# First stage of a hybrid decoder layer: weight splits before swaps and step sizes, V in side banks, stores issued by SyncE

## The reference

```
h = rmsnorm(x) * norm_pre
z, xbc, dt_raw, q, k, v, g_att, b, c, hs, g_sc = split(h @ w_in)
dt = softplus(dt_raw + dt_bias); a_cum = cumsum(dt * -exp(a_log))      # step sizes, 32 heads
k, q = rope(k), rope(q)                                                # 4 key heads, 16 query heads
y_att = window_attention(q, cache_k + k, cache_v + v, sinks) * silu(g_att)
y_ssd = chunked_scan(conv(xbc), dt, a_cum, state) ...
y_sc  = b * conv3(c * hs) * silu(g_sc)
x += rmsnorm(concat(y) @ w_out) * norm_post
x += sigmoid(x @ ple_gate) * (p @ ple_proj)
outputs: x, new conv and scan states, the last 128 keys and values of each sequence
```

## Time and profile before

| | |
|---|---|
| median of 3 runs | 2210.95 us (2208.93 to 2211.19) |
| the profiled execution | 2206.55 us |
| its span, first to last instruction | 2204.7 us |
| TensorE busy | 2108.5 us, 96% |
| VectorE busy | 1404.4 us, 64% |
| ScalarE busy | 1088.7 us, 49% |
| mean granted TensorE clock | 0.985 of full speed |
| memory traffic | 169 GB/s over the span |

### The profile page before, as it was taken

One profiled execution on the slowest core, in us unless ns is written; L12 is line 12 of the kernel. 1 busy time (PEld: TensorE's weight loads), 2 busy tenths in 40 slices (PEclk: granted clock), 3 DMA queues, 4 the chain that ended last, 5 costly groups with the idle time before them and its releaser, 6 DMA issues.

```text
span 2204.7 us, 39574 instructions
## 1 busy us (share of the span) xinstructions
PE 2108.5 (96%) x15750; PEld 2044.0 (93%) x15750; DVE 1404.4 (64%) x2329; ACT 1088.7 (49%) x2151; POOL 53.7 (2%) x141
## 2 busy tenths in 40 slices
PE   4899999999999999999968999999999999999999
PEld 3899999999999989999968999999999998999999
DVE  5476677577677674347564667676776776644575
ACT  4456456446455454345444564563564464533543
POOL 0000000001001000000000000000000000000000
PEclk9999999999999999999989999999999999999999
DMA  5645455455455355554536455454554553555544
GB/s 199 189 138 174 159 182 174 152 180 176 135 204 166 127 198 182 179 175 153 170 121 194 144 164 184 157 174 159 182 174 158 183 178 116 200 179 179 170 154 148
DMA packets 146369, 370.94 MB, mean 168 GB/s; under 512 B 28584, under 2 KB 65256, under 8 KB 144744
## 3 DMA queue, kind: packets, MB, share of 16 engines
q1 hardware_dynamic: 133552, 336.39, 46.3%
q10 hardware_dynamic: 12488, 29.65, 3.9%
q0 software_dynamic: 144, 2.36, 0.3%
HBM read 340.41 MB, written 32.01 MB: 169 GB/s over the span
## 4 chain that ended last, share of the span: by engine, by line
PE 80%; DVE 7%; DMA 5%; ACT 3%; DVEq 2%; SPq 1%; issue 1%; ACTq 1%
PE main L461 24%; PE main L463 23%; PE main L462 23%; DMA raw<-wts 4%; PE yo L587 2%; DVE wlo L1168 1%; PE yb L580 1%; DVE conv_sum L1402 1%; DMA ssm_p<-work 1%; PE yo L585 1%; DVEq L1200 1%; PE t L664 1%; ACTq L804 1%; DVEq L1290 1%; DVEq L1579 1%
## 5 line engine op out<-in xcount | busy, mean ns | idle before, releaser
L461 PE MATMUL main<-h_hi,whi 128*128 128x288 f32 x3952 | 1193.6, 302 | 55.4 <-DVE work L1198 18.6
L462 PE MATMUL main<-h_lo,whi 128*128 128x288 f32 x3952 | 1175.0, 297 | 0.0
L463 PE MATMUL main<-h_hi,wlo 128*128 128x288 f32 x3952 | 1170.8, 296 | 0.0
L1168 DVE TENSOR_TENSOR wlo<-raw,whi 128x1024 fp32r<-128x1024 f32 x568 | 691.8, 1222 | 451.6 <-ACT whi L786 438.7
L461 PEld LDWEIGHTS main<-h_hi,whi 128*128 128x128 f32 x3952 | 749.9, 190 | 77.0 <-issue 28.8
L786 ACT ACTIVATE whi<-raw 128x1024 fp32r<-128x1024 f32 x568 | 577.5, 1053 | 379.9 <-DMA raw<-wts 214.2
L462 PEld LDWEIGHTS main<-h_lo,whi 128*128 128x128 f32 x3952 | 751.5, 190 | 4.2 <-issue 2.7
L463 PEld LDWEIGHTS main<-h_hi,wlo 128*128 128x128 f32 x3952 | 752.8, 190 | 0.0
L1402 DVE SCALAR_TENSOR_TENSOR conv_sum<-conv_in,gpar_sb,conv_sum 128x312 f32<-128x312 f32 x144 | 90.2, 626 | 119.3 <-ACT conv_sum L948 111.3
L462 PE MATMUL main<-yssd_lo,whi 128*128 128x288 f32 x512 | 151.1, 295 | 0.0
L463 PE MATMUL main<-yssd_hi,wlo 128*128 128x288 f32 x512 | 150.9, 295 | 0.0
(11 more groups left out here) (271 smaller groups left out, 1819.1 us busy)
## 6 DMA issues: line engine op xcount, KB each, us to landing
raw<-wts SPq DMA_DIRECT2D x568, 512.0 KB, 3.6
work<-s_t SPq DMA_DIRECT2D x32, 512.0 KB, 6.0
ssm_s<-work ACTq DMA_DIRECT2D x8, 2048.0 KB, 8.0
work<-masks SPq DMA_DIRECT2D x8, 720.0 KB, 4.8
y_or_x<-xs SPq DMA_DIRECT2D x16, 288.0 KB, 4.3
xs<-y_or_x ACTq DMA_DIRECT2D x2, 2016.0 KB, 7.5
y_or_x<-x SPq DMA_DIRECT2D x4, 576.0 KB, 5.5
xs<-y_or_x POOLq DMA_DIRECT2D x1, 2304.0 KB, 7.6
```

The costliest lines, as they stand in the source:

```text
L461: mm(out, w_hi, x_hi_, start=start, stop=False)
L462: mm(out, w_hi, x_lo_, start=False, stop=False)
L463: return mm(out, w_lo, x_hi_, start=False, stop=stop)
L1168: return tt(dst, raw, hi.bitcast(F32), ALU.subtract)
```

## The change

TensorE: units 2 and 3 go to the side banks YB and YO, which the turned V tiles use after them; the main banks pass from K straight to group 0's first two units. ScalarE: halves 5, 6 and 7 are split before it waits for the K pair; then come both swaps, then the halves 8 to 12 with the steps and the V copies between them. VectorE: low parts 4 to 7 first, then both rotations, then the whole of `step_sizes`, then low part 8 and what follows. The K stores, V stores and cache copies are issued by SyncE: K stores after group 0's second unit has been loaded, V stores after the fourth, cache copies after unit 8 of group 1. In group 0 the keys come from `KTT` in SBUF instead of memory, without the waits for `k_stored` and `tok_ready`, one unit earlier; values are loaded after k = 5 there. The step buffers move to where the attention's PR begins, `RST` to the start of the attention region and `HF` behind the step-size weights.

```diff
--- before.py
+++ after.py
@@ -199,21 +199,22 @@
         NM = cut(16)
         DEN = cut(16)
         OS = cut(2 * NSM).rearrange("p (a n) -> p a n", n=NSM)
+        PR_AT = at[0]
         PR = cut(4 * 3 * P).rearrange("p (j n) -> p j n", j=4)
         PS = cut(NB * P + NSM)
         PT = cut(4 * 3 * P).rearrange("p (j n) -> p j n", j=4)
         PTS = cut(9 * P)
 
         XSQ = cut(KT * T, 0)
-        DT0 = cut(T, HEAVY + 2400)
+        RST = cut(T, HEAVY)
+        HF = [cut(T) if i else cut(T, KT * T + DTW) for i in range(6)]
+        DT0 = cut(T, PR_AT)
         AC0 = cut(T)
         W0 = cut(T)
         DTR = cut(T)
         DTE = cut(T)
         DTU = cut(T)
         DTC = cut(T)
-        RST = cut(T)
-        HF = [cut(T) for _ in range(6)]
         assert at[0] <= LATE
         KTT = cut(2 * T, LATE).rearrange("p (t n) -> p t n", n=T)
         KSW = cut(2 * T).rearrange("p (t n) -> p t n", n=T)
@@ -225,7 +226,7 @@
         YLO = post.enter_context(nc.sbuf_tensor("yssd_lo", [P, KT * T], F32R))
         MIX = post.enter_context(nc.sbuf_tensor("mix", [P, KT * T], F32))
         DTRAW = post.enter_context(nc.sbuf_tensor("dt_raw", [P, DTW], F32))
-        assert 3 * KT * T + DTW <= WK_N and LATE >= 2 * KT * T + 7 * T and 2 * KT * T + UNIT - KT * T <= HEAVY + 2400
+        assert 3 * KT * T + DTW <= WK_N and LATE >= 2 * KT * T + 7 * T and 2 * KT * T + UNIT - KT * T  <= WK_N
         PRAW = YX[:, KT * T:KT * T + 2 * T]
 
         COS, SIN = CST[:, C_COS:C_COS + T], CST[:, C_SIN:C_SIN + T]
@@ -255,7 +256,7 @@
                 return L * self.per + (self.pre + G * self.grp + n + 1)
 
         A0, A1 = Bank("a0", 0, 10, 3), Bank("a1", 0, 9, 3)
-        YB, YO = Bank("yb", 1, 7, 3), Bank("yo", 1, 7, 2)
+        YB, YO = Bank("yb", 2, 7, 3), Bank("yo", 2, 7, 2)
         T0, T1 = Bank("t0", 2, 8, 1), Bank("t1", 1, 8, 2)
         BANKS = {"A0": A0, "A1": A1, "T0": T0, "T1": T1}
         SIDE = [A0, A1, YB, YO, T0, T1]
@@ -318,7 +319,7 @@
         def gunit(L, g, k):
             return L * LAYER_U + g * GRP_U + (PRE_U + k)
 
-        OUT_F = PRE_U // 2 + G * GRP_U // 2
+        OUT_F = 1 + G * GRP_U // 2
         E_F = OUT_F + KT // 2
         GATE_F = E_F + 2
 
@@ -392,18 +393,32 @@
                 for g in range(0, G):
                     for k in range(GRP_U):
                         load_unit(gunit(L, g, k))
-                        if k == (1 if g else 2):
+                        if g == 0 and k == 1:
+                            sp.wait_ge(k_ready, L * 2 + 2)
+                            for i in range(2):
+                                sp.dma_start(kout[L, 2 * i:2 * i + 2].rearrange("h d n -> (h d) n"), KTT[:, i, :]).then_inc(k_stored, 16)
+                        if g == 0 and k == 3:
+                            sp.wait_ge(v_tok, L * 2 + 2)
+                            for i in range(2):
+                                for h in range(2):
+                                    v_h = VT[:, i, :].rearrange("p (c h d) -> p c h d", c=3, h=2)[:, :, h, :]
+                                    sp.dma_start(vout[L, 2 * i + h, 0:NPR].rearrange("(c p) d -> p c d", p=P), v_h[:, 0:2]).then_inc(v_stored, 16)
+                                    sp.dma_start(vout[L, 2 * i + h, NPR:T], v_h[0:NSM, 2]).then_inc(v_stored, 16)
+                        if g == 1 and k == 8:
+                            sp.dma_start(kold[L], kc_t[L].rearrange("g d (b w) -> (g d) b w", w=P)[:, :, NS:P]).then_inc(old_copied, 16)
+                            sp.dma_start(vold[L], vc_t[L][:, NS:P, :]).then_inc(old_copied, 16)
+                        if k == 1:
 
                             if L + g > 0:
                                 sp.wait_ge(y_sq, it(L, g - 1, 3, 2))
                             sp.wait_ge(s1_stored, L * (G * 16) + g * 16 + 16)
-                            sp.wait_ge(k_stored, L * 32 + 32)
-                            sp.wait_ge(tok_ready, L + 1)
+                            if g > 0:
+                                sp.wait_ge(k_stored, L * 32 + 32)
                             for r in range(2):
-                                sp.dma_start(KCUR[64 * r:64 * r + 64, :], kout[L, g]).then_inc(att_in, 16)
+                                sp.dma_start(KCUR[64 * r:64 * r + 64, :], kout[L, g] if g else KTT[0:64, 0, :]).then_inc(att_in, 16)
                             sp.dma_start(KC[0:64, :], kc_t[L, g]).then_inc(att_in, 16)
                             sp.dma_start(MSK, masks).then_inc(msk_in, 16)
-                        if k == 3:
+                        if k == (3 if g else 5):
 
                             sp.wait_ge(v_stored, L * 128 + 128)
                             sp.dma_start(VC, vc_t[L, g].rearrange("w (b d) -> w b d", d=HD)).then_inc(val_in, 16)
@@ -503,13 +518,19 @@
                     mm(T1.t[:, 0:T], w, HLO[:, c0:c0 + T], start=False, stop=False)
                     last = mm(T1.t[:, 0:T], wl, HHI[:, c0:c0 + T], start=False, stop=(n == KT - 1))
                 last.then_inc(T1.full, 1)
-                for k in (2, 3):
-                    project(unit(L, k), k % 2, fill(L, k % 2, k // 2))
+                for k, bk in ((2, YB), (3, YO)):
+                    wait(bk.free, bk.in_pre(L, 0))
+                    for n in range(KT):
+                        wait_half(unit(L, k), n)
+                        last = product(bk.t[:, 0:T], unit(L, k), n, HHI, HLO, n, n == 0, n == KT - 1)
+                        if n % 8 == 7:
+                            last.then_inc(halves_used, 1)
+                    pe.sem_inc(bk.full, 1)
 
                 def turn_values(i):
                     bk = (YB, YO)[i]
                     wait(v_ready, L * 2 + (i + 1))
-                    wait(bk.free, bk.in_pre(L, 0))
+                    wait(bk.free, bk.in_pre(L, 1))
                     for c in range(3):
                         n = P if c < 2 else NSM
                         last = tr(bk.t[0:n, c * P:c * P + P], VTT[:, i, c * P:c * P + n], ID)
@@ -589,7 +610,7 @@
                         last.then_inc(YO.full, 1)
 
                     for k in range(GRP_U):
-                        project(gunit(L, g, k), k % 2, fill(L, k % 2, (PRE_U + g * GRP_U + k) // 2))
+                        project(gunit(L, g, k), k % 2, fill(L, k % 2, 1 + (g * GRP_U + k) // 2))
                         if k < 2 and g > 0:
                             late_states(g - 1, k)
                         if g == 0 and k == 0:
@@ -825,14 +846,20 @@
                     fn(HHI[:, i * T:(i + 1) * T], HF[i % 6], ACT.Copy).then_inc(h_hi, 1)
                 act.wait_ge(layer_in, L * 64 + 64)
                 fn(DTP[0:32, 2:3], DTP[0:32, 1:2], ACT.Exp)
-                for k in range(PRE_U):
-                    act.wait_ge(halves_used, used(unit(L, k)))
-                    if k < 2:
-                        swap(KSW[:, k, :], MAIN[k % 2]).then_inc(k_swapped, 1)
-                    else:
-                        fn(VTT[:, k - 2, :], MAIN[k % 2][:, 0:T], ACT.Copy).then_inc(v_ready, 1)
-                        act.drain().then_inc(bank_free[k % 2], 1)
-                    split_after(unit(L, k))
+                def keep_values(i):
+                    bk = (YB, YO)[i]
+                    act.wait_ge(halves_used, used(unit(L, 2 + i)))
+                    fn(VTT[:, i, :], bk.t[:, 0:T], ACT.Copy).then_inc(v_ready, 1)
+                    act.drain().then_inc(bk.free, 1)
+
+                first_half = 2 * unit(L, 0)
+                for h in (5, 6, 7):
+                    split_hi(first_half + h)
+                act.wait_ge(halves_used, used(unit(L, 1)))
+                for k in range(2):
+                    swap(KSW[:, k, :], MAIN[k]).then_inc(k_swapped, 1)
+                for k in range(4):
+                    split_hi(first_half + 8 + k)
                     if k == 0:
 
                         act.wait_ge(dt_abs, L + 1)
@@ -840,6 +867,9 @@
                         act.wait_ge(dt_u, L + 1)
                         fn(DTC[0:32, :], DTU[0:32, :], ACT.Ln).then_inc(dt_ln, 1)
                     if k == 1:
+                        keep_values(0)
+
+                    if k == 2:
 
                         act.wait_ge(ac_ready, L + 1)
                         fn(AC3[0:32, :], AC0[0:32, :], ACT.Copy).then_inc(ac_hi, 1)
@@ -848,21 +878,15 @@
                         fn(AC3[32:64, :], DTR[0:32, :], ACT.Copy).then_inc(ac_mid, 1)
                         act.wait_ge(dt_ac, L + 1)
                         fn(W0[0:32, :], DTE[0:32, :], ACT.Exp, scale=-1.0).then_inc(dt_wexp, 1)
-                    if k == 2:
-                        for i in range(2):
-                            act.wait_ge(k_ready, L * 2 + (i + 1))
-                            act.dma_start(kout[L, 2 * i:2 * i + 2].rearrange("h d n -> (h d) n"), KTT[:, i, :]).then_inc(k_stored, 16)
+                    if k == 3:
+                        keep_values(1)
+                        split_hi(first_half + 12)
 
                 def store_values(i):
                     bk = (YB, YO)[i]
```

(26 more changed lines are left out.)

## The result

Four runs of the changed kernel gave a median of 2196.80 us (2195.25 to 2197.92), four of the kernel before beside them 2211.07 (2208.93 to 2213.00): a ratio of 0.9935, interval 0.9918 to 0.9952. It is faster by 14.3 us, not by 32.6, and 2196.8 lies above the range of 2172 to 2192.

The account below looks back on a forecast made before the run. TensorE was taken as the bound, busy 2108.5 of 2204.7 us. Gains of 15.9 us in layer 0 and 16.7 in layer 1, together 32.6, took 2206.55 to 2174.0, or 2178.4 on the median's footing; range 2172 to 2192.

Parts of the forecast that it names:

- V in side banks: First stage, both layers: units 2 and 3 no longer wait for the main banks; the 4.04 and 1.72 us go.
- the step chain: First stage: step sizes end at 61.5, the product about 67.6, against the turn at 70.3; cost nothing.
- half 8: Group 0's first unit: weight half ready at 62.7, wanted by TensorE at 63.9; slack 1.2 us, the tightest place.
- Rival A: First stage: half 8 late behind the step sizes, 2 to 4 us per layer, 2182 to 2186; chance 0.16.
- B: First scores: ScalarE still late through weight halves queued behind loads and stores; 6 us per layer stay, 2190; chance 0.12.
- Stores to SyncE: Before group 0's first scores: ScalarE's 6.1 us of issue goes, so the 5.32 us gap goes too.
- a part worth nothing: If moving the stores wins nothing: ScalarE 2 to 4 us late for the second swap, time 2182 to 2186.
- Cache copies: Group 1: next half issued at 303.2 lands near 309, harmless until 318.8; ScalarE may wait 1 to 2 us; cost nothing.
- Rival D: Unit 9 of group 1: cache copies starve the weight ring, 18.5 us per layer, 2215 and up; chance 0.04.
- The last sign: First stage: a time above 2192 would mean that a queue, not TensorE, sets it.
- Group 0's keys on chip: Group 0: keys on chip replace a round trip through memory and a wait; counted as nothing.
- the moved buffers: Buffers moved to other places carry no instruction; counted as nothing.

Follow-up runs that it names:

- the GpSimd run: The changed kernel with its two cache copies issued by GpSimd on its own queue instead of SyncE, same place in group 1; 2201.39 us, ratio 0.9962 to the kernel before.

## Why the prediction was wrong

**V in side banks, the step chain, half 8: right.** Half 8's low part was made from 61.6 on (forecast 61.5), unit 2 and unit 3 ran without a gap at clock 1.00, the steps were turned at 70.36 (forecast 70.3), the scores came at 84.52 (84.5), the fourth unit at 85.38 (85.3). Rival A and B had no part. The answering rows of VectorE and SyncE after:

```profile
61.62 2.34 DVE L1189 TENSOR_TENSOR wlo<-raw,whi 128x1024 fp32r<-128x1024 f32 x2
```

```profile
78.75 0.90 SPq L368 DMA_DIRECT2D raw<-wts  x2
```

Half 16 was issued at 78.75, as forecast ("about 79"), and was in time.

**Stores to SyncE: right in time, wrong in cause.** The 5.32 us before the scores did go. I put them down to ScalarE's 6.1 us of issue; with the same issue time back on ScalarE the kernel loses 1.4 us in all, and with the value copy cut otherwise those waits shrink in the old kernel by 3.6 and 4.7 us of 5.32 and 6.16, all its stores still on ScalarE. The issue took the 6 us that I read, but it stood beside other work; most of the wait was the value copy's. My price for a part worth nothing, 4 to 8 us, was too high as well.

**Cache copies: the step that failed.** They were put at "cost nothing" in group 1 and cost 8.1 and 8.5 us. "It would land near 309, behind them", 5.8 us after its issue at 303.2; it landed 15.7 us after, issued at 286.89 in a kernel that was 17 us ahead by then. The two ends stood in the text (309, and 318.8 as the latest harmless moment), and nothing supported the first: the old place of the copies showed a landing of 11.9 us, and I gave it to the masks in front. It landed about at my own limit, at 302.6 against 318.8 - 17.3 = 301.5 (302.9 with the gain of 15.9 that I forecast), which would cost 1.1 us or nothing, and still 8 us were lost per layer, for the limit was the wrong one. I asked only when TensorE needs the half. Other work stands behind its split on ScalarE and VectorE, and the sampled probabilities were due at 303.2, 4.6 us before they were begun. "ScalarE may wait 1 to 2 us there" was 12.2 us.

**Rival D** had the place right and even its threshold ("decisive when first half lands more than 15.6 us after its issue"), but by that threshold a half that lands after 15.7 us costs 0.1 us, and 18.5 us per layer needs 34; and its reason, whole copies ahead in one ring, fell with the GpSimd run. The missing 18.3 us (32.6 - 14.3) are 16.6 of this wait; the rest is within what single runs differ by. Of the two profiled executions, on which the sum was made, more is missing: 2197.0 against its 2174.0. There the changed kernel lost, beside the wait, another 6.1 us between layer 0's turn, 9.2 us ahead, and layer 1's pair, 1142.04 - 1138.94 = 3.1 us ahead, with no wait of TensorE that the old kernel lacks; the last section shows where half of it went.

**The last sign** was wrong too: the time is above 2192, yet no queue sets the first stage, which ran as forecast.

**Group 0's keys on chip and the moved buffers** were costed at nothing, and no wait of the profile after contradicts it; they were not tried alone.

## What to carry to other kernels

Before moving a large transfer, look at its shape: of two copies of 992 KB the one with 4 entries in its slowest dimension took twice as long (17.2 us against 8.8) and held up weight loads beside it, whether SyncE or GpSimd issued it, and cut otherwise it cost next to nothing. When you ask whether a late load matters, don't stop at its consumer: list what stands behind the waiting instruction in each engine's program, and when TensorE wants each of those. And when a transfer must be moved into a full stretch, move it in pieces, and look for what made the old place slow before you credit the removal.

## What the runs showed of the hardware that was not expected

The granted clock also falls where TensorE has no idle gap. In the stage of the groups' scan, with its many matmuls of 4 columns, the same work in two kernels (it runs 2.3 us later in the one with the copies in pieces): the changed kernel first, the one with the copies in pieces behind it.

```profile
199.00:205.00 6.00, 6.00 (x37) 4.86 (x34) 5.13 (x12) 5.07 (x17) 0.00 (x0) 0.72 0.27 87
```

```profile
201.00:207.00 6.00, 6.00 (x50) 5.31 (x49) 5.03 (x12) 5.41 (x18) 0.00 (x0) 1.00 0.27 87
```

TensorE is busy for all 6.00 us in both, but at a mean clock of 0.72 it starts 37 matmuls, and at 1.00 it starts 50; the difference is (50 - 37)/50 x 6.00 = 1.6 us. The same stretch can be followed through group 1's scan of layer 0, between the same two matmuls: the kernel before, then the changed one.

```profile
380.17:400.39 20.22, 20.22 (x164) 18.99 (x163) 11.20 (x23) 12.33 (x37) 0.00 (x0) 1.00 0.30 104
```

```profile
370.95:394.28 23.33, 23.33 (x164) 21.54 (x163) 11.19 (x23) 12.33 (x37) 0.00 (x0) 0.85 0.29 91
```

The same 164 matmuls took 3.1 us more at a mean clock of 0.85, with no gap in either. Such stretches come in some groups of a kernel and not in others, without a change in the code there. That fits a spread like that of the cut value copy, 2173.13 to 2183.07, the 5.4 us between the kernel without copies and the one in pieces, and that the two profiled executions differ by 9.5 us where the medians differ by 14.3 (mean clock 0.985 and 0.982). What starts such a stretch stays open; no run was made for it.
